# Two hybrid transformer blocks in one launch: the last value products and the transposes of the attention output are placed elsewhere in the order of the work

## The reference, cut to what matters

```
# first kind of mixer (three attentions, each with a branch weight and a gate)
y_a = o_a @ w_branch[:256];  y_b = o_b @ w_branch[256:512];  y_c = o_c @ w_branch[512:]
merged = sigmoid(ga) * y_a + sigmoid(gb) * y_b + sigmoid(gc) * y_c
return merged @ w_out
# second kind (a state-space branch and a latent attention)
merged = g[..., :1024] * y_ssd + g[..., 1024:] * y_mla
h = h + merged @ w_o
```

## Time and profile before

| | |
|---|---|
| median of 3 executions | 2789.8 us (2786.63 to 2793.22) |
| the profiled execution, its own time | 2786.49 us |
| its span, first to last instruction | 2784.7 us |
| mean granted TensorE clock | 0.991 |
| PE busy | 2721.8 us, 98% |
| DVE busy | 1483.6 us, 53% |
| ACT busy | 1345.4 us, 48% |
| POOL busy | 662.4 us, 24% |
| HBM read | 458.09 MB |

### The profile page before, as it was taken

How to read it: one execution, slowest core, us unless ns; L and a number is a source line. 1 busy time by engine, 2 the same in 40 slices (tenths; PEclk the granted TensorE clock), 3 DMA queues, 4 the chain that set the end, 5 groups by cost and what they waited for, 6 DMA issues and landing times.

```text
span 2784.7 us, 32279 instructions
## 1 busy us (share of the span) xinstructions
PE 2721.8 (98%) x12892; PEld 2237.3 (80%) x12892; DVE 1483.6 (53%) x2246; ACT 1345.4 (48%) x1559; POOL 662.4 (24%) x153
## 2 busy tenths in 40 slices
PE   8999999999999999999999999999999999999999
PEld 7888778888887778888887787788888887877887
DVE  3438773333458763433358885443334488864433
ACT  4335664334345654343356574443433464744432
POOL 4330014444420023343410000043444100000333
PEclk9999999999999999999999999999999999999999
DMA  6554435556554345555544244355555542442553
GB/s 227 190 181 163 151 124 195 181 178 204 183 170 161 135 138 196 184 181 195 184 166 157 76 156 160 123 182 182 181 198 178 190 145 86 152 155 105 186 189 135
DMA packets 209928, 461.23 MB, mean 166 GB/s; under 512 B 9458, under 2 KB 31604, under 8 KB 209780
## 3 DMA queue, kind: packets, MB, share of 16 engines
q1 hardware_dynamic: 209780, 459.17, 48.5%
HBM read 458.09 MB, written 1.05 MB: 165 GB/s over the span
## 4 chain that ended last, share of the span: by engine, by line
PE 84%; DVE 9%; ACT 4%; issue 3%; POOL 0%; DMA 0%; DVEq 0%; ACTq 0%; SPq 0%
PE banks L322 26%; PE banks L324 25%; PE banks L323 25%; PE banks L416 3%; DVE w_lo L261 2%; ACT w_hi L285 2%; PE banks L659 2%; DVE xbcT L1718 1%; PE banks L682 1%; PE banks L1425 1%; PE banks L1439 1%; PE banks L671 0%; ACT h_hi L446 0%; DVE h_lo L460 0%; POOL w_lo L261 0%
## 5 line engine op out<-in xcount | busy, mean ns | idle before, releaser
L285 ACT ACTIVATE w_hi<-raw 128x2048 fp32r<-128x2048 f32 (+1 forms) x441 | 832.9, 1889 | 1151.4 <-PE banks L324 1102.5
L261 POOL TENSOR_TENSOR w_lo<-raw,w_hi 128x2048 fp32r<-128x2048 f32 (+1 forms) x141 | 648.0, 4596 | 1725.5 <-ACT w_hi L285 1725.5
L261 DVE TENSOR_TENSOR w_lo<-raw,w_hi 128x2048 fp32r<-128x2048 f32 (+1 forms) x300 | 692.8, 2314 | 609.7 <-ACT w_hi L285 602.7
L322 PE MATMUL banks<-w_hi,h_lo 128*128 128x512 f32 x2336 | 924.6, 396 | 13.5 <-DVE w_lo L261 6.3
L324 PE MATMUL banks<-w_hi,h_hi 128*128 128x512 f32 x2336 | 909.1, 389 | 0.0
L323 PE MATMUL banks<-w_lo,h_hi 128*128 128x512 f32 x2336 | 908.5, 389 | 0.0
L322 PEld LDWEIGHTS banks<-w_hi,h_lo 128*128 128x128 f32 x2336 | 441.9, 189 | 116.7 <-issue 16.2
L324 PEld LDWEIGHTS banks<-w_hi,h_hi 128*128 128x128 f32 x2336 | 441.1, 189 | 91.2
L323 PEld LDWEIGHTS banks<-w_lo,h_hi 128*128 128x128 f32 x2336 | 441.7, 189 | 84.6
L322 PE MATMUL banks<-w_hi,act_lo 128*128 128x512 f32 x704 | 276.3, 392 | 0.9 <-POOL w_lo L261 0.9
L324 PE MATMUL banks<-w_hi,act_hi 128*128 128x512 f32 x704 | 274.4, 390 | 0.0
(11 more groups left out here) (272 smaller groups left out, 2544.7 us busy)
## 6 DMA issues: line engine op xcount, KB each, us to landing
raw<-in_ffn_w SPq DMA_DIRECT2D x124, 1024.0 KB, 5.0
raw<-in_w_in SPq DMA_DIRECT2D x108, 1024.0 KB, 5.0
raw<-in_ffn_w_down SPq DMA_DIRECT2D x44, 1024.0 KB, 4.8
raw<-in_ffn_w_gate SPq DMA_DIRECT2D x40, 1024.0 KB, 5.0
raw<-in_ffn_w_up SPq DMA_DIRECT2D x40, 1024.0 KB, 5.0
raw<-in_w_ssd_out SPq DMA_DIRECT2D x16, 1024.0 KB, 4.9
raw<-in_w_branch SPq DMA_DIRECT2D x8, 1024.0 KB, 4.8
raw<-in_w_out SPq DMA_DIRECT2D x8, 1024.0 KB, 4.8
```

Source lines behind the costliest of these rows:

```text
L261: eng.tensor_tensor(w_lo[:, c % SPLIT, 0:kc * n], raw[:, c % RAW, 0:kc * n], w_hi[:, c % SPLIT, 0:kc * n].bitcast(F32), ALU.subtract).then ...
L285: self.eng.activation(w_hi[:, c % SPLIT, 0:kc * n], raw[:, c % RAW, 0:kc * n], ACT.Copy).then_inc(hi_made, 1)
L322: pe.matmul(ps, al, bh, start=first, stop=False)
```

## The change

All of it is in the order of the work and in which banks are used; no arithmetic is added or left out.

- **First kind, PE.** oT1 is transposed in step 14, into the bank of gate product 4. oT2 and oT3 move to after half 0 of ya's chunk, into banks 2 and 3. Value product 15 moves into yb's first half, between its two token tiles; oT0 follows the second tile. `deep` gets `mids`, a table of what is to be called after which (half, tile).
- **First kind, ACT.** gate(5) moves behind value products 13, 14 and 15; oT1's copy moves into step 15; oT0's copy and the sigmoids of gate a move ahead of the copies of oT2 and oT3, with a chunk copy (index 28) in between; the sigmoids of gate c follow them.
- **First kind, DVE.** oT1's low part comes ahead of the scaling of o_c; those of oT2 and oT3 come after the first half of ya is gated; two explicit calls for low parts of chunks (indices 26 and 27) go, so that they are made when the next read makes them due.
- **Second kind, PE.** oT0 and oT1 are transposed in step 7, into a pair of product banks. Value product 7 and oT2 move into ym's first half, between its tiles; oT3 stays after ym's first chunk.
- **Second kind, ACT.** gate(1) moves behind value products 5 and 6; oT0 and oT1 are copied in step 7.
- **Second kind, DVE.** In each half of ym both gating products come first, then both additions.
- **Bank pairs.** A counter (`banks.pair`) says with which pair of banks a stage starts, so that the longest unused pair is first; so, ym and wo of the second kind follow it by `flip`.

```diff
@@ deep
+                    if mids and k0 == 0 and (half, i) in mids:
+                        mids[half, i]()
...
-                if mid and k0 == 0:
-                    mid()
@@ ffn_pe
-            start_bank = 2 if f == 0 else 0
-            banks.next["g"] = start_bank
+            start_bank = banks.next["g"] = banks.pair
+            banks.pair ^= 2
@@ mix1_pe
+                if s == STEPS1 - 2:
+                    for n in range(4):
+                        banks.was_read(pe, f"pv{n}")
+                    turn_o(1, banks.at[banks.key("gg4.0")][0])
             finish(gate_steps[5])
...
-            for s in range(4):
-                banks.was_read(pe, f"pv{s}")
-            turn_o(1, 4)
             turn_pe(pe, banks, STEPS1 - 1, steps[STEPS1 - 1])
             values_pe(pe, banks, STEPS1 - 2, steps[STEPS1 - 2])
-            pe.wait_ge(*banks.of(laid, 4))
-            turn_o(2, 5)
-            values_pe(pe, banks, STEPS1 - 1, steps[STEPS1 - 1])
-            turn_o(3, 6)
...
+            def last_values():
+                values_pe(pe, banks, STEPS1 - 1, steps[STEPS1 - 1])
...
+            def turn_long():
+                pe.wait_ge(*banks.of(laid, 4))
+                turn_o(2, 2)
+                turn_o(3, 3)
...
-            finish(deep(pe, banks, chunks, "yb", o(2), 2, 0, ready(2), mid=turn_last, flip=1))
-            finish(deep(pe, banks, chunks, "ya", o(0), 2, 4, ready(0)))
+            finish(deep(pe, banks, chunks, "yb", o(2), 2, 0, ready(2), flip=1,
+                        mids={(0, 0): last_values, (0, 1): turn_first}))
+            finish(deep(pe, banks, chunks, "ya", o(0), 2, 4, ready(0), mids={(0, 1): turn_long}))
@@ mix1_act
-                if s == STEPS1 - 1:
-                    gate(5)
                 if s >= 2:
                     values_act(spa, banks, s - 2, steps[s - 2])
...
-            high_turned(spa, "oT1", o_hi, 2)
+                if s == STEPS1 - 1:
+                    high_turned(spa, "oT1", o_hi, 2)
+            values_act(spa, banks, STEPS1 - 1, steps[STEPS1 - 1])
+            gate(5)
+            high_turned(spa, "oT0", o_hi, 0)
...
+            sigmoid(0)
+            spa.upto(m0 + 28)
             subg = lambda k: SUBG
             high_turned(spa, "oT2", o_hi, 4, subg)
             high_turned(spa, "oT3", o_hi, 6, subg)
-            values_act(spa, banks, STEPS1 - 1, steps[STEPS1 - 1])
-            high_turned(spa, "oT0", o_hi, 0)
...
+            sigmoid(2)
@@ mix1_dve
+            low_turned(spv, "oT1", o_hi, o_lo, 2)
...
             dve.sem_inc(laid, 1)
-            lo(26)
-            low_turned(spv, "oT1", o_hi, o_lo, 2)
-            low_turned(spv, "oT2", o_hi, o_lo, 4, subg)
-            low_turned(spv, "oT3", o_hi, o_lo, 6, subg)
-            lo(27)
...
+                if half == 0:
+                    low_turned(spv, "oT2", o_hi, o_lo, 4, subg)
+                    low_turned(spv, "oT3", o_hi, o_lo, 6, subg)
@@ mix2_pe
                 if s == STEPS2:
                     finish(gate_steps[1])
-                    turn_o(0)
-                    turn_o(1)
...
-            values_pe(pe, banks, STEPS2 - 1, steps[STEPS2 - 1])
+                if s == STEPS2 - 1:
+                    turn_o(0, pair)
+                    turn_o(1, pair + 1)
+
+            def last_values():
+                values_pe(pe, banks, STEPS2 - 1, steps[STEPS2 - 1])
+                turn_o(2, 4)
@@ mix2_act
                 if s < STEPS2:
+                    if s >= STEPS2 - 2:
+                        spa.upto(m0 + 41 + s)
...
-                if s == STEPS2 - 1:
-                    gate(1)
                 if s >= 2:
                     values_act(spa, banks, s - 2, steps[s - 2])
+                if s == STEPS2 - 1:
+                    high_turned(spa, "oT0", o2_hi, 0)
+                    high_turned(spa, "oT1", o2_hi, 2)
+            gate(1)
@@ mix2_dve
+                if s >= STEPS2 - 1:
+                    lo(40 + s)
...
                     v.link_read(dve.tensor_tensor(m2[:, i, part], ps, gates2[:, i, part], ALU.mult), read)
+                for i in range(TT):
                     v.link(dve.tensor_tensor(ys[:, i, part], ys[:, i, part], m2[:, i, part], ALU.add))
```

More of the change, by code:

```diff
@@ L190, in __init__ @@
                 self.layer = 0
+                self.pair = 2
                 self.makers = makers
@@ L367, in finish, with deep @@
                 pass
-        def deep(pe, banks, chunks, name, lhs, kt, bank0=0, ready=None, between=None, mid=None, flip=0):
+        def deep(pe, banks, chunks, name, lhs, kt, bank0=0, ready=None, between=None, mids=None, flip=0):
             bank = lambda half, i: bank0 + 2 * (half ^ flip) + i
@@ L848, in mix1_pe @@
             h = (h_hi, h_lo)
+            assert banks.pair == 0
             banks.next["g"] = 0
@@ L883, in mix1_pe, with turn_o @@
                 banks.was_read(pe, f"tr{j}")
+            def turn_o(j, bank):
+                turn(pe, banks, f"oT{j}", [lambda i, k=k: o1[:, i, k * P:(k + 1) * P] for k in (2 * j, 2 * j + 1)], bank=bank)
             steps = steps1()
@@ L949, in mix1_pe, with mix1_act @@
                         between=lambda: norm_pe(pe, banks, 2, "wo", (0, 1), bank0=4)))
-        def mix1_act(spa, banks):
+        def mix1_act(spa, banks, m0):
             act = spa.eng
@@ L1029, in mix1_act, with sigmoid @@
                         value_squares(s - 2, steps[s - 2])
-            high_turned(spa, "oT1", o_hi, 2)
-            subg = lambda k: SUBG
-            high_turned(spa, "oT2", o_hi, 4, subg)
-            high_turned(spa, "oT3", o_hi, 6, subg)
+                if s == STEPS1 - 1:
+                    high_turned(spa, "oT1", o_hi, 2)
             values_act(spa, banks, STEPS1 - 1, steps[STEPS1 - 1])
+            gate(5)
             high_turned(spa, "oT0", o_hi, 0)
-            for g in (0, 2):
+            def sigmoid(g):
                 for i in range(TT):
@@ L1042, in mix1_act @@
                     act.activation(part, part, ACT.Sigmoid).then_inc(gates_done, 1)
+            sigmoid(0)
+            spa.upto(m0 + 28)
+            subg = lambda k: SUBG
+            high_turned(spa, "oT2", o_hi, 4, subg)
+            high_turned(spa, "oT3", o_hi, 6, subg)
+            sigmoid(2)
             for j in range(4):
@@ L1334, in mix2_pe @@
             h = (h_hi, h_lo)
-            banks.next["g"] = 0
+            banks.next["g"] = banks.pair
+            banks.pair ^= 2
+            pair, flip = banks.pair, banks.pair // 2
             ready = h_ready(pe, banks, 1)
@@ L1456, in mix2_pe @@
                 finish(product(pe, banks, chunks, f"gm{j}", h, KD))
-            so = deep(pe, banks, chunks, "so", (y_hi, y_lo), KI2, ready=lambda k: banks.was_read(pe, f"yT{k // 2}"), flip=1)
+            so = deep(pe, banks, chunks, "so", (y_hi, y_lo), KI2, ready=lambda k: banks.was_read(pe, f"yT{k // 2}"), flip=flip)
             for _ in range(5):
@@ L1470, in mix2_pe, with turn_o @@
                     banks.was_read(pe, f"qk{m}{p}")
-            def turn_o(j):
-                for s in (2 * j, 2 * j + 1):
-                    banks.was_read(pe, f"pv{s}")
-                turn(pe, banks, f"oT{j}", [lambda i, k=k: o2[:, i, k * P:(k + 1) * P] for k in (2 * j, 2 * j + 1)], bank=4 + j)
+            def turn_o(j, bank):
+                for n in (2 * j, 2 * j + 1):
+                    banks.was_read(pe, f"pv{n}")
+                turn(pe, banks, f"oT{j}", [lambda i, k=k: o2[:, i, k * P:(k + 1) * P] for k in (2 * j, 2 * j + 1)], bank=bank)
             steps = steps2()
@@ L1509, in first_half @@
                 turn_m(1)
-            finish(deep(pe, banks, chunks, "ym", (o2_hi, o2_lo), KD, ready=ready_o, between=first_half))
+            finish(deep(pe, banks, chunks, "ym", (o2_hi, o2_lo), KD, ready=ready_o, between=first_half, mids={(0, 0): last_values}, flip=flip))
             def ready_m(k):
@@ L1518, in ready_m @@
                     banks.was_read(pe, f"mT{k // 2}")
-            finish(deep(pe, banks, chunks, "wo", (m2_hi, m2_lo), KD, ready=ready_m,
+            finish(deep(pe, banks, chunks, "wo", (m2_hi, m2_lo), KD, ready=ready_m, flip=flip,
                         between=lambda: norm_pe(pe, banks, 2, "wo", (0, 1))))
@@ L1908, in mix2_dve @@
             for half in range(2):
+                part = slice(512 * half, 512 * half + 512)
                 for i in range(TT):
@@ L1911, in mix2_dve @@
                     dve.wait_ge(*banks.of(gates_done, i + 1))
-                    part = slice(512 * half, 512 * half + 512)
                     v.link_read(dve.tensor_tensor(m2[:, i, part], ps, gates2[:, i, part], ALU.mult), read)
+                for i in range(TT):
                     v.link(dve.tensor_tensor(ys[:, i, part], ys[:, i, part], m2[:, i, part], ALU.add))
```

18 lines of the change are left out of this document (7 added, 11 removed).

## The result

The changed kernel takes 2770.88 us (median of 4, 2767.85 to 2771.14) where the kernel before takes 2789.82 us: a ratio of 0.9928 (95% interval 0.9916 to 0.994), 18.9 us less. The forecast was 2770. Two further sets of runs of the same kernel gave 2768.79 and 2769.44 us, with ratios of 0.9925 and 0.9924; against the kernel before in the same rounds (2790.24 and 2790.71 us) that is 21.4 and 21.3 us less.

The account below looks back on a forecast made before the run. PE, busy 98% of the span, was bounded by its waits and the low clock behind them. Gains of 10.0, 8.3 and 1.4 us gave 19.7, so 2789.8 - 19.7 = 2770 us, range 2764 to 2780.

Parts of the forecast that it names:

- Sum: All terms together: 10.0 us in the first kind, 8.3 in the second, 1.4 for the additions; 19.7 us in all.
- the four stretches: PE's work after the last attention step of each layer; at most 22.3 us lost there to waits and low clock.
- gate evictions behind the values: ACT: two evictions of 0.67 us leave the path to bank 7, with no wait added for them.
- E + 3.2 us: When PE could start the last value product, counted from the gate product's end E.
- last value product inside: PE: value product inside the first output product, behind six matmuls; about 1.0 us of waiting left, where it was 2.3 to 3.3.
- the page of waits: Profile sign: PE's waits for L734 fall from 11.2 us to about 4, in one wait per layer.
- Clock: Granted clock 1.00 behind the waits; rival that it falls all the same (17%): 2781 us, or 2774 or 2777 for one kind.
- oT2 and oT3 inside ya: First kind: transposes moved at no PE cost, copied some 14 us after E; counted as nothing, bounds 0 to 1.5 us per layer.
- Both gating products first: Second kind, DVE: a 0.69 us addition leaves wo's path; wait falls from 1.9 to 1.2 us per layer, 1.4 for both.
- Bank pairs: Each stage starts with the pair read first, which lets gate(1) move back; no instruction added, counted as nothing.
- No gain is given back later: After the stretches PE runs as fast as chunks come, as before, so nothing takes the gain back later.

Follow-up runs that it names:

- e1: The changed kernel with ACT again emptying the last gate product's banks (gate(5), gate(1)) ahead of the value product two steps back; 2792.6 us, ratio 1.0013.
- e7: The changed kernel with ACT's last transposed probabilities and value product ahead of the due chunk copy, and DVE's oT0 and oT1 low parts ahead of the chunk's; 2767.2 us.
- e3: The changed kernel with the last value product back ahead of yb or ym instead of inside; 2781.8 us, ratio 0.9974.
- e5: The changed kernel with DVE's additions of ym back between the two gating products; 2772.5 us against 2768.8 for the changed kernel in the same rounds.
- e6: The changed kernel with the bank pairs of ym and wo exchanged, so ym's half 0 uses the last gate product's pair; 2784.5 us, ratio 0.998.
- e8: The changed kernel run again unchanged, as base for other runs in the same rounds; 2768.8 us.
- e10: The changed kernel run again unchanged, as base of e9 in the same rounds; 2769.4 us.
- e9: The kernel of e7 with DVE also gating both tiles of ym's second half before making the due chunk's low part; 2764.8 us, ratio 0.9911 to the kernel before.
- e2: The kernel before with only the evictions of gate(5) and gate(1) moved behind the value products, PE's order as before; 2780.6 us, ratio 0.9966.

## Why the prediction was right

**Sum.** Predicted 19.7 us; the four stretches gave 18.6 and the medians 18.9. First kind: 4.8 and 5.2 predicted, 4.5 and 4.9 measured. Second kind: 4.1 and 0.7, 4.2 and 0.7 predicted, 4.6 and 4.6 measured.

**gate evictions behind the values.** Right, and the necessary part: without it nothing is left (e1). My words for it were too narrow: I named two evictions of 0.67 us, but in the earlier trace rows only one stands behind the end of the gate product, and bank 7 came free 3.5 us earlier, counted from that end, because the value product of step 13 now stands ahead of the chunk copy too. E + 3.2 us for the last value product came out: E is 376.13 (the gate product's end, where the transposes start) and the value product starts at 379.35. The evictions ended at 382.14, as did the transposes of oT0, and yb's second half began at 382.28, E + 6.15 instead of 5.87: that is the missing 0.3 us of the first kind. Half of it lies in front of this half of yb, the other half in small steps between the last value product and here. yb itself began at 377.24 instead of 377.0, but that only took from the wait behind it.

**last value product inside.** Right in size: about 1.0 us between starts was left; the sixth matmul starts at 378.48, so the next could at 378.7, and it is 379.35, after 0.65 us, plus those 0.25 ahead of yb. What I wrote of the page of waits was off: I said about 4 us would stay for L734, in one wait per layer, and it is 1.1 in three. I had put a distance between starts in the place of idle time: a matmul's modelled end lies 0.39 us after its start, the next start 0.23, so that each idle figure is 0.16 short; and a part of the time stands elsewhere, ahead of yb in the first kind and at ym's start in the second, for `o_lo` (0.5), as I had worked out for DVE. The size is borne out by e7, which removes these waits and gains 0.7 us per layer of the first kind and 1.1 of the second, 3.6 in all.

**Clock.** Right: granted 1.00 in all four stretches. That the clock was part of the price is shown by e3, with the same wait at either level. The Trainium skill, "TensorE: Matmul & The Clock Gate", "A second HAM failure mode: psum-queue depth-cycling", tells of a kernel whose frequent short idles between groups of matmuls made the clock swing. Here waits of 0.5 us and less left it up in all four stretches; waits of 2.2 and 2.3 us (e3) lowered it in three of four.

**oT2 and oT3 inside ya.** Right, and close: ACT ended their copies at 388.58 + 1.57 = 390.15, 14.0 us after E; no wait for a low part of a chunk showed in yc. The table load is followed by its sigmoid at once (382.96 + 1.28 to 384.25), so the draining of about 1380 ns in the Trainium skill, "ScalarE: Activation LUTs", "What ACT_TABLE_LOAD costs", is not seen here either.

**Both gating products first.** Right: 1.1 us left where 1.2 were said, and e5 puts 0.7 us per layer on the order.

**Bank pairs.** Right that they cost nothing that shows: behind the last stretch both kernels take 207.4 us. They are what makes the later gate(1) possible: the wrong pair costs 8.3 us at ym and 7.4 at the feed-forward behind it (e6).

**No gain is given back later.** True of the change. But the two profiled executions differ by only 15.4 us, 2786.49 to 2771.09 us; the missing 3.2 us lie in layer 1's projections (1.2), in the second mixers' first parts (0.8 and 1.0) and ahead of the first stretch (0.2, the load of x). In layer 1's projections the clock differs from one execution to the next of one kernel (e8, e10), and in the second mixers runs with the same code there (e5, e7) do not lose the time, so this is chance. I had not allowed for it in the step from one profile to the median. The profiled execution came at 2771.09 us and not at the 2766.8 worked out for it; the median fell within 1 us of the forecast because this profile lies 0.2 us above its median where that of the kernel before lies 3.3 below. So the closeness is in part luck: the stretches gave 1.1 us less than the sum, and the later sets of runs gave 1.6 to 1.7 more.

## What to carry to other kernels

When a dense engine idles for a short time, read its clock behind the wait: here 2.3 us of idle time cost 5.8, and the change paid 18.6 us where the waits that it touches fell by 10.7 in the table. Look at what stands in the releasing engine's queue between the wanted instruction and the one before: evictions that nobody waits for belong behind the one that holds the wanted bank, above all when they must themselves wait for a product to end. A chunk copy that is due by rule is such a guest too (e7), and on DVE its low part (e9). And compare stretches between the same two instructions, not only totals: in the changed kernel, with the clock up, they repeated to 0.1 us where the whole program varies by 3 us.

## What the runs showed of the hardware that I had not expected

An idle time of the same length lowers the clock in one layer and not in another of the same execution: 2.2 to 2.3 us in e3 (three of four), 1.8 us in e5 (layer 2 and not layer 3). The wait at the same place in wo was 1.8 us in e2, where the level fell both times, and 1.9 us in the kernel before, where it stayed up both times. In the stretches measured here the shortest waits behind which the level fell were 1.8 us; 1.3 us in e2 left it up both times. What decides between them is open. The price is known: with the clock down, the same wait cost 1.4 to 1.7 us more in e3, and in e1, behind a wait of 2.7 us, PE stayed at the low level for some 10 us in layer 0.

Stretches of low clock in untouched code came and went between executions of one kernel. How much of the spread of its times they make is not settled. Executions of the kernel before with a mean granted clock of 0.988 took 2790.6 to 2792.1 us and those with 0.993 took 2786.4 to 2787.2, but those with 0.991 lie anywhere from 2786.5 to 2792.9.
